# The RWKV layer's triangular inverse as a loop on TensorE, with its transposed copies made by products with the identity

## The reference

```python
def step(s, inp):
    r_t, w_t, k_t, v_t, a_t, b_t = inp
    sa = jnp.einsum('bhij,bhj->bhi', s, a_t)
    s = s * w_t[:, :, None, :] + sa[..., None] * b_t[:, :, None, :] + v_t[..., None] * k_t[:, :, None, :]
    return s, jnp.einsum('bhij,bhj->bhi', s, r_t)
```

## Time and profile before

| | us |
|---|---|
| median of 3 runs | 2439.85 |
| lowest, highest | 2438.2, 2440.07 |
| the profiled execution | 2445.84 |
| its span in the trace | 2444.0 |

### The profile page before, as it was taken

How to read it: one execution, slowest core, us unless ns; L and a number is a source line. 1 busy time by engine, 2 the same in 40 slices (tenths; PEclk the granted TensorE clock), 3 DMA queues, 4 the chain that set the end, 5 groups by cost and what they waited for, 6 DMA issues and landing times.

```text
span 2444.0 us, 53999 instructions
## 1 busy us (share of the span) xinstructions
PE 2282.3 (93%) x20594; PEld 2214.1 (91%) x20594; DVE 1293.9 (53%) x1881; ACT 1025.5 (42%) x1513; POOL 1899.5 (78%) x1388
## 2 busy tenths in 40 slices
PE   6999999999999899999999788679999999999997
PEld 6999989999998789999999587558999999998997
DVE  5752147725752336744771866745771773335762
ACT  4344344344344435344343543224443434445442
POOL 6997828997996618897997696746898899755996
PEclk9999999999999989999999689998999999999999
DMA  5554524554553304564554132012555455432563
GB/s 181 179 195 133 183 67 146 173 197 130 179 193 122 129 18 148 177 202 127 172 189 163 69 112 87 4 38 95 172 187 173 146 172 198 142 125 95 181 197 111
DMA packets 89950, 348.84 MB, mean 143 GB/s; under 512 B 9968, under 2 KB 11760, under 8 KB 89712
## 3 DMA queue, kind: packets, MB, share of 16 engines
q1 hardware_dynamic: 89840, 347.31, 44.3%
HBM read 346.22 MB, written 1.05 MB: 142 GB/s over the span
## 4 chain that ended last, share of the span: by engine, by line
PE 76%; POOL 11%; issue 6%; DVE 4%; ACT 3%; DMA 0%; POOLq 0%; SPq 0%; DVEq 0%; ACTq 0%
PE bank L306 23%; PE bank L308 22%; PE bank L307 22%; POOL w_lo L1325 7%; POOL h L1351 2%; PE bank L662 2%; POOL x_lo L1364 1%; ACT w_hi L938 1%; PE bank L573 1%; DVE m L1543 1%; PE bank L574 0%; DVE zneg L1618 0%; DVE zraw L1614 0%; ACT zexp L1077 0%; PE bank L445 0%
## 5 line engine op out<-in xcount | busy, mean ns | idle before, releaser
L1325 POOL TENSOR_TENSOR w_lo<-raw,w_hi 128x512 fp32r<-128x512 f32 (+4 forms) x1155 | 1699.1, 1505 | 419.1 <-ACT w_hi L938 396.5
L306 PE MATMUL bank<-x_hi,w_hi 128*128 128x272 f32 (+1 forms) x3312 | 971.5, 293 | 34.3 <-POOL x_lo L1364 12.8
L308 PE MATMUL bank<-x_hi,w_lo 128*128 128x272 f32 (+1 forms) x3312 | 961.8, 290 | 0.0
L307 PE MATMUL bank<-x_lo,w_hi 128*128 128x272 f32 (+1 forms) x3312 | 960.5, 290 | 0.0
L938 ACT ACTIVATE w_hi<-raw 128x1024 fp32r<-128x1024 f32 (+2 forms) x608 | 666.9, 1116 | 265.0 <-PE bank L308 242.7
L306 PEld LDWEIGHTS bank<-x_hi,w_hi 128*128 128x128 f32 x3312 | 630.7, 190 | 48.7 <-issue 24.9
L307 PEld LDWEIGHTS bank<-x_lo,w_hi 128*128 128x128 f32 x3312 | 631.8, 191 | 0.2
L308 PEld LDWEIGHTS bank<-x_hi,w_lo 128*128 128x128 f32 x3312 | 631.7, 191 | 0.0
L306 PE MATMUL bank<-hid_hi,w_hi 128*128 128x272 f32 (+1 forms) x1408 | 404.1, 287 | 0.0
L308 PE MATMUL bank<-hid_hi,w_lo 128*128 128x272 f32 (+1 forms) x1408 | 403.7, 287 | 0.0
L307 PE MATMUL bank<-hid_lo,w_hi 128*128 128x272 f32 (+1 forms) x1408 | 403.0, 286 | 0.0
(11 more groups left out here) (293 smaller groups left out, 2370.4 us busy)
## 6 DMA issues: line engine op xcount, KB each, us to landing
raw<-in_ffn_in SPq DMA_DIRECT2D x352, 512.0 KB, 3.5
raw<-in_ffn_out SPq DMA_DIRECT2D x128, 704.0 KB, 4.0
raw<-in_sb_in SPq DMA_DIRECT2D x48, 512.0 KB, 3.5
raw<-in_rw_in SPq DMA_DIRECT2D x24, 512.0 KB, 3.3
raw<-in_sb_out SPq DMA_DIRECT2D x16, 512.0 KB, 3.5
raw<-in_mla_out SPq DMA_DIRECT2D x8, 512.0 KB, 3.2
raw<-in_rw_lora SPq DMA_DIRECT2D x8, 512.0 KB, 4.7
raw<-in_rw_out SPq DMA_DIRECT2D x8, 512.0 KB, 3.4
```

The lines of the kernel that those rows point to most:

```text
L306: nc.tensor.matmul(o, wh, xh[:, k, cols()], start=start, stop=False)
L307: nc.tensor.matmul(o, wh, xl[:, k, cols()], start=False, stop=False)
L308: last = nc.tensor.matmul(o, wl, xh[:, k, cols()], start=False, stop=stop)
L1325: part = nc.gpsimd.tensor_tensor(w_lo[:, s, w], raw[:, s, w], w_hi[:, s, w], ALU.subtract)
```

## The change

TensorE's program of the inverse becomes a part ahead, a loop and a part behind. Ahead: `Y` of level 1 for the four pairs and `Z` of level 1 for the first two, and the key-value items of pairs 2 and 3 (that of pair 2 stood in `grams`). The loop runs over levels 2 to 5; for each pair it issues `Y`, a new item `T`, and `Z` of the pair two steps back. `T` multiplies each block of `inv` as the stationary operand with the 64 x 64 identity, which gives the transpose of the inverse in PSUM with the halves already changed. Its even bank is copied to `tinv` by VectorE (`turned`), its odd bank by ScalarE, in place of the three transposes on VectorE. Behind the loop stand `Z` of the last two pairs. All items in the loop have five chunks; copies and sums keep the widths of before. The waits in the loop are against values that are computed from the loop's counter, and each group of them is followed by an increment of a semaphore (`turn_taken`) that nobody waits for. The other engines stay written out, in the new order.

```diff
--- before.py
+++ after.py
@@ -231,7 +231,7 @@
-        state_carried, inside_done = sem("state_carried"), sem("inside_done")
+        state_carried, inside_done, turn_taken, turned_done = (sem(n) for n in ("state_carried", "inside_done", "turn_taken", "turned_done"))
@@ -656,6 +656,10 @@
                 claim(X)
                 claim(X + 1)
                 core_at[key, p] = X, uses[X], uses[X + 1], counts[name]
+                products(X, p, done, come_from, go_to, left, right, total)
+                counts[name] += 2
+
+            def products(X, p, done, come_from, go_to, left, right, total=NCH):
                 for T in range(total):
                     for at, (j, e) in enumerate(heads_of(p)):
                         s, f = slot_of(j, e), come_from(j, e)
@@ -663,7 +667,6 @@
                                                 start=T == 0, stop=T == total - 1)
                         if at % 2 and T == total - 1:
                             last.then_inc(done, 1)
-                counts[name] += 2
 
             def landed(key, p):
 
@@ -695,7 +698,7 @@
                     if p == 0:
                         pe.wait_ge(ops_ready, 2)
                     gram("Rb", p, a_, r_)
-                    if p:
+                    if 0 < p < PAIRS - 1:
                         key_values(p - 1)
                     if p == 0:
                         pe.wait_ge(ops_ready, 3)
@@ -705,30 +708,81 @@
 
             def inversion():
 
-                steps_ = [(lv, p) for lv in range(1, LEVELS) for p in range(PAIRS)]
-
-                def first_half(lv, p):
-
-                    pe.wait_ge(aml_ready, 2 * (PAIRS * (lv - 1) + p) + 2)
-                    if lv == 1:
-                        pe.wait_ge(inv0_ready, 2 * p + 2)
-                    else:
-                        landed(("Z", lv - 1), p)
-                    item(("Y", lv), p, y_done, "y", at_tokens, at_features, lambda f, j, s, T: aml[f, s, cc(T)], lambda f, j, s, T: inv[f, s, cc(T)], chunks_of(lv))
+                into_y = lambda: (at_tokens, at_features, lambda f, j, s, T: aml[f, s, cc(T)], lambda f, j, s, T: inv[f, s, cc(T)])
+                into_z = lambda: (at_features, at_tokens, lambda f, j, s, T: tinv[f, s, cc(T)], lambda f, j, s, T: yl[f, s, cc(T)])
 
                 def second_half(lv, p):
-
                     landed(("Y", lv), p)
-                    pe.wait_ge(tinv_ready, 2 * (p + 1) if lv == 1 else 2 * PAIRS + 3 * (PAIRS * (lv - 2) + p + 1))
-                    item(("Z", lv), p, z_done, "z", at_features, at_tokens, lambda f, j, s, T: tinv[f, s, cc(T)], lambda f, j, s, T: yl[f, s, cc(T)], chunks_of(lv))
-
-                for g in range(len(steps_) + 2):
-                    if g < len(steps_):
-                        first_half(*steps_[g])
-                    if g == 2:
-                        key_values(PAIRS - 1)
-                    if g >= 2:
-                        second_half(*steps_[g - 2])
+                    pe.wait_ge(tinv_ready, 3 * (PAIRS * (lv - 1) + p + 1))
+                    item(("Z", lv), p, z_done, "z", *into_z())
+
+                into_t = lambda: (at_tokens, at_features, lambda f, j, s, T: inv[f, s, cc(T)], lambda f, j, s, T: ident64[f, :])
+
+                for p in range(PAIRS):
+                    pe.wait_ge(aml_ready, 2 * p + 2)
+                    pe.wait_ge(inv0_ready, 2 * p + 2)
+                    item(("Y", 1), p, y_done, "y", *into_y())
+                    if p == 2:
+                        key_values(2)
+                        second_half(1, 0)
+                    if p == 3:
+                        key_values(3)
+                        second_half(1, 1)
+
+                first_item, base = counts["item"], list(uses)
+                place = {("Y", p): 3 * p for p in range(PAIRS)}
+                place.update({("T", p): 3 * p + 1 for p in range(PAIRS)})
+                place.update({("Z", p): 3 * ((p + 2) % PAIRS) + 2 for p in range(PAIRS)})
+                bank_at = lambda k: 2 * ((first_item + k) % 4)
+                claims = lambda k, lv, odd=0: 3 * lv + (base[bank_at(k) + odd] + k // 4 - 5)
+                for lv in range(1, LEVELS):
+                    for p in range(PAIRS):
+                        for name in "YZT" if lv > 1 else "ZT" if p >= 2 else "T":
+                            k, of = place[name, p], lv + (name == "Z" and p >= 2 or name == "T")
+                            X = bank_at(k)
+                            core_at[(name, lv), p] = X, claims(k, of), claims(k, of, 1), 2 * (PAIRS * (lv - 1) + p)
+
+                def claim_at(k, lv):
+                    for odd in range(2):
+                        pe.wait_ge(bank_free[bank_at(k) + odd], claims(k, lv, odd))
+
+                def landed_at(k, lv):
+                    for odd in range(2):
+                        pe.wait_ge(bank_free[bank_at(k) + odd], claims(k, lv, odd) + 1)
+
+                def z_of(lv, p, within):
+
+                    landed_at(place["Y", p], within)
+                    landed_at(place["T", p], lv)
+                    claim_at(place["Z", p], lv if p < 2 else lv + 1)
+                    pe.sem_inc(turn_taken, 1)
+                    products(bank_at(place["Z", p]), p, z_done, *into_z())
+
+                pe.wait_ge(tinv_ready, 3 * PAIRS)
+                with pe.Fori(2, LEVELS) as lv:
+                    for p in range(PAIRS):
+                        pe.wait_ge(aml_ready, 2 * PAIRS * lv + 2 * (p + 1 - PAIRS))
+                        landed_at(place["Z", p], lv - 1 if p < 2 else lv)
+                        claim_at(place["Y", p], lv)
+                        pe.sem_inc(turn_taken, 1)
+                        products(bank_at(place["Y", p]), p, y_done, *into_y())
+                        claim_at(place["T", p], lv)
+                        pe.sem_inc(turn_taken, 1)
+                        products(bank_at(place["T", p]), p, turned_done, *into_t())
+                        if p < 2:
+                            z_of(lv - 1, p + 2, lv - 1)
+                        else:
+                            z_of(lv, p - 2, lv)
+                for b in range(8):
+                    uses[b] += 3 * (LEVELS - 2)
+                counts["item"] += 12 * (LEVELS - 2)
+                counts["y"] += 2 * PAIRS * (LEVELS - 2)
+                counts["z"] += 2 * PAIRS * (LEVELS - 2)
+                for p in (2, 3):
+                    last_level = LEVELS - 1
+                    landed(("Y", last_level), p)
+                    landed(("T", last_level - 1), p)
+                    item(("Z", last_level), p, z_done, "z", *into_z())
 
             def half_heads(H):
 
@@ -1246,15 +1300,19 @@
                     evacuate("tv", p, tok_done, lambda s: tv[:, s, :])
                 for p in range(PAIRS):
                     evacuate("tb", p, tok_done, lambda s: tb[:, s, :])
-                    if p:
+                    if 0 < p < PAIRS - 1:
                         evacuate("akv", p - 1, akv_done, lambda s: akv[:, s, :])
                     evacuate("tk", p, tok_done, lambda s: tk[:, s, :])
                 for lv in range(1, LEVELS):
                     width = TC * chunks_of(lv)
                     for p in range(PAIRS):
+                        if lv == 1 and p >= 2:
+                            evacuate("akv", p, akv_done, lambda s: akv[:, s, :])
                         evacuate(("Y", lv), p, y_done, lambda s: yl[:, s, 0:width], chunks_of(lv))
-                        if (lv, p) == (1, 2):
-                            evacuate("akv", PAIRS - 1, akv_done, lambda s: akv[:, s, :])
+                        if lv > 1:
+                            X, _, _, base = core_at[("T", lv - 1), p]
+                            act.wait_ge(turned_done, base + 2)
+                            nc.scalar.activation(tinv[:, 2 * p + 1, 0:width], bank[X + 1][:, 0:width], ACT.Copy).then_inc(bank_free[X + 1], 1)
                 act.wait_ge(z_done, 2 * PAIRS * (LEVELS - 1))
                 for c in range(NCH):
                     if c:
@@ -1817,7 +1875,7 @@
                         nc.vector.transpose(inv[:, s, :], tinv[:, s, :]).then_inc(inv0_ready, 1)
                     dve.wait_ge(inv0_ready, 2 * p + 2)
                     for side in range(2):
-                        nc.vector.transpose(tinv[half_at(1 - side), 2 * p + 1, :], inv[half_at(side), 2 * p + 1, :]).then_inc(tinv_ready, 1)
+                        nc.vector.transpose(tinv[half_at(1 - side), 2 * p + 1, :], inv[half_at(side), 2 * p + 1, :]).then_inc(tinv_ready, 1 + side)
 
                 for p in range(PAIRS):
                     masked("A", p, lambda s: am[:, s, :], m_lower)
@@ -1829,24 +1887,26 @@
                 level0(PAIRS - 1)
 
             def inverse_steps():
+
+                def turned(lv, p):
+                    X, _, _, base = core_at[("T", lv), p]
+                    w = slice(0, TC * chunks_of(lv + 1))
+                    dve.wait_ge(turned_done, base + 1)
```

(17 more changed lines are left out.)

## The result

| | before | after |
|---|---|---|
| median of 7 runs each, us | 2439.85 | 2448.74 |
| lowest, highest | 2437.84, 2441.16 | 2444.60, 2450.65 |
| ratio of after to before, with its 95% interval | | 1.0036 (1.0026 to 1.0045) |
| profiled execution and its span | 2445.84, 2444.0 | 2449.23, 2447.4 |

A forecast was written before the change was run, and what follows sets the result against it. Instruction fetch on TensorE was taken to pace the inverse. Terms 9.1 + 16.1 + 30 + 2.0 gave 57.2 us against 48.8, +8.4, less 1.1 behind it: +7.3, so 2447 us; range 2436 to 2462, 0.8 inside.

The forecast's parts named there:

- The forecast's case: Changed inverse: turns of 9 to 13 us, slower by 7.3 us, 2447 us (2444 to 2456), chance 0.56.
- What bounds it: Triangular inverse before: paced by instruction fetch, 256 TensorE instructions per 4.0 us, 49.6 us computed against 48.8 in the trace.
- Two limits close together: Inverse before: VectorE, busy 40.5 of 49 us, lies almost on the fetch limit, so relieving one alone gives little.
- The loop stays: Loop over levels 2 to 5: its four or five pieces stay in the engine, so later turns run without fetch.
- Rival A: Loop does not stay resident: turns 2 to 4 fetched again, 18 to 30 us above forecast, 2471 us, chance 0.14.
- The turn: One loop turn from resident code: 12 items of 0.58 us plus 0.25 us for waits, 10 us, ends 7.0 and 13.
- rival B: Loop waits hidden behind the matmuls: a turn costs 7.0 us, change -1.7 us, 2438 us, chance 0.22.
- ahead of the loop, less the moved item: Code before the loop, paced by fetch: 664 less 80 instructions at 4.0 us per 256, 9.1 us.
- first turn: Loop's first turn, paced by fetch: 1030 instructions at 4.0 us per 256, 16.1 us.
- three turns: Loop's remaining turns, run from resident code at 10 us each, 30 us.
- behind the loop, last adds: Two items after the loop and the last adds, 2.0 us; the present last burst to the adds' end is 1.4.
- taken back behind the stage: Fetch gap of 1.14 us before the recurrence: the next piece is there after the loop, so 1.1 us is saved.

The follow-up runs named there:

- two kernels like it: The changed kernel with each bank wait of the loop doubled, 2455.0 us; and with fewer waits and `T` only for the odd slot, 2439.2 us.

## Why the prediction was right

The forecast's case happened, its sign and its size.

**What bounds it.** Right, and it was the step that decided. The view by stretch pointed at VectorE (40.5 of 49 us); the count of matmuls between two stops and the instruction queue pointed at fetch. Taking 11 us of work off VectorE changed nothing, making the code 1586 instructions longer cost 22 us.

**Two limits close together.** Right, and closer than it said: without fetch VectorE takes over at 8.8 us a turn (the loop without `T`), and before did its levels 2 to 4 in 11.0, 8.7 and 8.4 us.

**The loop stays.** Right in this kernel; 7 pieces in the inverse, about 8 forecast, and one in the last 30 us of the loop instead of none. Rival A named a real edge, at a larger body than this one.

**The turn.** 12 x (0.58 + 0.25) = 10 us; measured 10.04. The terms hold too: 0.58 is the spacing in the earlier trace rows, and `Y` to `T`, with two waits, came to 0.61. The 0.25 was a choice between 0 and 0.5, with no row behind it but two gaps; that it came out so near is luck. The runs with fewer and doubled waits show that it was mostly waits, so rival B (hidden) is out. It spreads unevenly, 0.03 to 0.09 us ahead of `T`, 0.2 to 0.4 ahead of `Y` and `Z`, and 0.8 at the loop's end.

**The sum**, term by term:

| | forecast, us | measured |
|---|---|---|
| ahead of the loop, less the moved item | 9.1 | 8.4 |
| first turn | 16.1 | 15.6 |
| three turns | 30 | 29.7 |
| behind the loop, last adds | 2.0 | 2.3 |
| sum | 57.2 | 56.0 |
| the inverse before | 48.8 | 48.8 |
| taken back behind the stage | 1.1 | 0.1 |
| change | +7.3 | +7.1 |

The measured column is from the chain above: first `Y` of the inverse at 1545.10 (timeline), of the loop at 1556.99, of the second turn at 1572.56, first item behind the loop at 1602.23, last add's end at 1604.52. The first `Y` came 28.0 us after the Gram part's first matmul, 31.5 before, so 3.5 us go off the 11.9 ahead of the loop. These are the rows of after, then of before:

```profile
1517.11 0.81 PE L666 MATMUL bank<-raw,a_ 64*64 64x64 f32 x40
...
1545.10 0.65 PE L666 MATMUL bank<-k_,aml 64*64 64x64 f32 x29
...
1520.52 0.81 PE L662 MATMUL bank<-raw,a_ 64*64 64x64 f32 x40
```

The first row of the table hides two misses that nearly cancel. At the forecast's price the 664 instructions ahead of the loop take 10.4 us and took 11.9, and the moved item's 80 take 1.25 off the Gram part, which lost 3.5. That they cancel is luck; why the Gram part gained more than its 80 instructions is open.

**Where it was off.** The gain of 1.1 us behind the stage did not come: after the last add TensorE waits 1.01 us on "issue", 1.14 before. The sentence "after a long stay in the loop the next piece is there" failed as a price, since the gap does not come from a missing piece alone: between 1572 and 1602 us after fetched a single one, and the wait is still there, as it is in the kernel with the loop and without `T` (1.04 us). What it is stays open. It was made good by terms that were 1.2 us too large. That the two errors cancel is luck, and the runs' own 8.9 us is 1.6 above the forecast, which their interval (6.3 to 11.0) allows.

## What to carry to other kernels

When an engine stops after the same number of instructions each time, in the middle of work that has no wait, count its instructions and look at its instruction queue: here a piece of 256 came every 4.0 us, and small float32 products use one up in 2.2. Such code is priced by its length, not by its busy time; making other engines lighter gives nothing, and moving work onto TensorE costs code. A loop takes the fetch away when its body stays in the engine (13 us here, against the same code written out), but then its turns have a price of their own: the waits against the counter and whatever the next bound is. With the transposes left on VectorE that bound lay where fetch had been, and the inverse got no shorter (49.3 against 48.8 us). So weigh a transfer of work between engines at the loop's pace, after the loop is in.

## What was not expected of the hardware

- An item with half the products, all on two of the four pairs of halves, was hardly cheaper: its 20 matmuls took 0.54 us, the 40 of a full item 0.58.
- A wait in the loop costs 0.05 to 0.07 us even when it is long satisfied; 52 of them, with the arithmetic and the branch, make 3.0 us of a 10.0 us turn.
- A loop body of some 1000 TensorE instructions was gone round three more times with one piece fetched in 30 us (none in two kernels like it); one of some 2080 was fetched again.
